# The last chunks of an RWKV-7 recurrence: state decayed ahead of its terms, and four steps in another order

## The reference, cut to what matters

```python
def step(state, inp):
    r_t, w_t, k_t, v_t, a_t, b_t = inp
    sa = jnp.einsum('bhvk,bhk->bhv', state, a_t)
    state = (state * w_t[:, :, None, :] + sa[..., None] * b_t[:, :, None, :]
             + v_t[..., None] * k_t[:, :, None, :])
    return state, jnp.einsum('bhvk,bhk->bhv', state, r_t)
...
y = rms_norm((b_gate * y).reshape(bsz, seq, CONV_GROUPS, HEAD_DIM), out_gain)   # short convolution
...
y = jnp.concatenate([y_rwkv, y_conv, y_attn], axis=-1)
x = x + y @ w_o[l]
```

## Time and profile before

| | us |
|---|---|
| median of 3 runs | 1580.93 |
| lowest, highest | 1580.54, 1581.57 |
| the profiled execution, its time | 1580.65 |
| the profiled execution, its span | 1578.8 |
| PE busy | 1555.1 (98%) |
| DVE busy | 1264.2 (80%) |
| ACT busy | 1073.8 (68%) |

### The profile page before, as it was taken

One profiled execution on the slowest core, in us unless ns is written; L12 is line 12 of the kernel. 1 busy time (PEld: TensorE's weight loads), 2 busy tenths in 40 slices (PEclk: granted clock), 3 DMA queues, 4 the chain that ended last, 5 costly groups with the idle time before them and its releaser, 6 DMA issues.

```text
span 1578.8 us, 28727 instructions
## 1 busy us (share of the span) xinstructions
PE 1555.1 (98%) x10958; PEld 1359.9 (86%) x10958; DVE 1264.2 (80%) x1440; ACT 1073.8 (68%) x1323; POOL 80.2 (5%) x82
## 2 busy tenths in 40 slices
PE   8999999999999998999999999999999999999997
PEld 8988999999999887888888888888888888888886
DVE  5686754444567866999999999999999999999996
ACT  5545444444446455788888888888888888888885
POOL 0022000000000400000000000000000000000000
PEclk9999999999999999999999999999999999999999
DMA  8700655555344008999999999999999999999994
GB/s 313 234 2 3 220 186 184 186 187 187 122 163 152 3 17 307 359 377 361 391 393 361 389 393 362 394 390 358 393 389 359 393 390 359 392 391 358 390 379 158
DMA packets 189944, 447.76 MB, mean 284 GB/s; under 512 B 8208, under 2 KB 10784, under 8 KB 189728
## 3 DMA queue, kind: packets, MB, share of 16 engines
q1 hardware_dynamic: 186480, 434.46, 75.5%
q0 software_dynamic: 2688, 9.44, 2.7%
q10 hardware_dynamic: 688, 2.62, 0.5%
HBM read 438.63 MB, written 6.29 MB: 282 GB/s over the span
## 4 chain that ended last, share of the span: by engine, by line
PE 96%; DVE 2%; ACT 1%; issue 1%; DMA 0%; POOL 0%; SPq 0%; DVEq 0%; ACTq 0%; POOLq 0%
PE bank L789 28%; PE bank L791 27%; PE bank L790 27%; PE bank L770 9%; PE bank L1465 2%; ACT w_hi L1544 0%; DMA ring<-in_w_in 0%; PE bank L960 0%; PE bank L810 0%; DVE w_lo L2239 0%; PE bank L1428 0%; PE bank L1214 0%; DVE w_lo L1986 0%; PE bank L1105 0%; POOL out L740 0%
## 5 line engine op out<-in xcount | busy, mean ns | idle before, releaser
L1544 ACT ACTIVATE w_hi<-ring 128x1024 fp32r<-128x1024 f32 x812 | 858.6, 1061 | 334.5 <-PE bank L791 324.5
L2239 DVE TENSOR_TENSOR w_lo<-ring,w_hi 128x1024 fp32r<-128x1024 f32 x672 | 814.4, 1224 | 62.6 <-ACT w_hi L1544 12.9
L789 PE MATMUL bank<-w_hi,acts_hi 128*128 128x512 f32 (+1 forms) x1376 | 539.7, 392 | 3.5 <-DVE w_lo L2239 3.4
L791 PE MATMUL bank<-w_hi,acts_lo 128*128 128x512 f32 (+1 forms) x1376 | 533.6, 388 | 0.0
L790 PE MATMUL bank<-w_lo,acts_hi 128*128 128x512 f32 (+1 forms) x1376 | 532.8, 387 | 0.0
L789 PEld LDWEIGHTS bank<-w_hi,acts_hi 128*128 128x128 f32 x1376 | 258.9, 188 | 55.4 <-DVE w_lo L2239 4.5
L791 PEld LDWEIGHTS bank<-w_hi,acts_lo 128*128 128x128 f32 x1376 | 258.7, 188 | 53.8
L790 PEld LDWEIGHTS bank<-w_lo,acts_hi 128*128 128x128 f32 x1376 | 259.1, 188 | 50.8
L789 PE MATMUL bank<-acts_hi,w_hi 128*128 128x256 f32 x884 | 252.4, 286 | 2.7 <-DVE acts_lo L2146 1.7
L790 PE MATMUL bank<-acts_lo,w_hi 128*128 128x256 f32 x884 | 250.1, 283 | 0.0
L791 PE MATMUL bank<-acts_hi,w_lo 128*128 128x256 f32 x884 | 250.1, 283 | 0.0
(11 more groups left out here) (247 smaller groups left out, 1112.6 us busy)
## 6 DMA issues: line engine op xcount, KB each, us to landing
ring<-in_moe_wg SPq DMA_DIRECT2D x112, 1024.0 KB, 7.1
ring<-in_moe_wu SPq DMA_DIRECT2D x112, 1024.0 KB, 7.5
ring<-in_moe_wd SPq DMA_DIRECT2D x112, 1024.0 KB, 7.1
ring<-in_w_in SPq DMA_DIRECT2D x24, 1024.0 KB, 7.8
ring<-in_dense_wg SPq DMA_DIRECT2D x14, 1024.0 KB, 5.2
ring<-in_dense_wu SPq DMA_DIRECT2D x14, 1024.0 KB, 5.1
ring<-in_dense_wd SPq DMA_DIRECT2D x14, 1024.0 KB, 4.9
ring<-in_w_o SPq DMA_DIRECT2D x8, 1024.0 KB, 7.7
```

Source lines behind the costliest of these rows:

```text
L789: pe.matmul(out_, a_hi, b_hi, start=first, stop=False, **kw)
L791: return pe.matmul(out_, a_lo, b_hi, start=False, stop=final, **kw)
L1544: return act.activation(o, i, ACT.Copy, **kw)
L2239: TT(w_lo[:, q, :], raw, w_hi[:, q, :].bitcast(F32), ALU.subtract).then_inc(lo_ready, 1)
```

## The change

The state is multiplied by its decay into `state_tmp` ahead of time (`decay_state`, before the add of u), and when the terms are there, three STTs, one for each pair of heads, make terms x decay + that product. `times_v(l, 5)` goes behind the b-u terms of border 2. The conv root goes from behind output_squares(4) to right behind the last exponentials, and its reciprocal from behind keep_output(5) to behind add_u(1). `spread_conv` writes bank 4 instead of bank 3 and no longer waits for `o_ready`; `scale_conv` reads there. `add_u(3)` goes ahead of `keep_output(l, 5)`. Nothing else is changed; the state's values are the same but for rounding.

```diff
@@ TensorE, recurrence @@
                 state_terms(2, tok_k, tok_v, True, False)
-                times_v(l, 5)
                 pe.wait_ge(u_ready, 3 * l + 2)
                 state_terms(2, tok_b, u_tok, False, True).then_inc(st_done, 1)
+                times_v(l, 5)
@@ TensorE, spread_conv @@
                 pe.wait_ge(conv_ready, l + 1)
-                pe.wait_ge(o_ready, HEADS * l + HEADS)
...
-                            last = mm(bank[3][e * HD:(e + 1) * HD, t * T + b * P:t * T + (b + 1) * P],
+                            last = mm(bank[4][e * HD:(e + 1) * HD, t * T + b * P:t * T + (b + 1) * P],
@@ ScalarE, recurrence @@
                 exponentials(l, 5)
+                act.wait_ge(conv_kept, l + 1)
+                act.activation(conv_rms, conv_rms, ACT.Sqrt).then_inc(conv_root, 1)
...
                 output_squares(l, 4)
-                act.wait_ge(conv_kept, l + 1)
-                act.activation(conv_rms, conv_rms, ACT.Sqrt).then_inc(conv_root, 1)
                 keep_cross(2)
@@ VectorE, recurrence @@
                     if c:
-                        then(TT(state_tmp, terms, state, ALU.add))
-                        TT(state, state_tmp, end, ALU.mult).then_inc(st_ready, 1)
+                        for i in range(NRT):
+                            last = STT(state[:, i, :], terms[:, i, :], w65[:, i, c, C:C + 1], state_tmp[:, i, :],
+                                       ALU.mult, ALU.add)
+                        last.then_inc(st_ready, 1)
...
+                def decay_state(c):
+                    dve.wait_ge(st_ready, 3 * l + c)
+                    then(TT(state_tmp, state, w65[:, :, c, C:C + 1].to_broadcast([P, NRT, HD]), ALU.mult))
...
-                               bank[3][:, i * T:(i + 1) * T], ALU.mult, ALU.mult)
+                               bank[4][:, i * T:(i + 1) * T], ALU.mult, ALU.mult)
 
                 state_update(0)
+                decay_state(1)
                 add_u(1)
+                dve.wait_ge(conv_root, l + 1)
+                dve.reciprocal(conv_rms, conv_rms).then_inc(conv_ready, 1)
                 state_update(1)
-                dve.wait_ge(st_ready, 3 * l + 2)
+                decay_state(2)
                 add_u(2)
                 state_update(2)
+                dve.wait_ge(st_ready, 3 * l + 3)
+                add_u(3)
                 keep_output(l, 5)
-                dve.wait_ge(conv_root, l + 1)
-                dve.reciprocal(conv_rms, conv_rms).then_inc(conv_ready, 1)
-                add_u(3)
                 scale_conv(0).then_inc(conv_out, 1)
```

## The result

| | us |
|---|---|
| before, median of 22 runs | 1580.96 (1579.49 to 1583.29) |
| changed, median of 22 runs | 1583.45 (1582.23 to 1585.85) |
| ratio | 1.0016, 95% interval 1.0009 to 1.0022 (1.4 to 3.5 us) |
| the profiled execution, its time and span | 1584.49, 1582.6 |

The account below looks back on a forecast made before the run. TensorE was taken to bound the kernel, carrying the chain for 96% of the span. The first output tile 0.39 us later in each of two layers gave +0.78, so 1581.7 against the 1580.93 median; range 1579.2 to 1583.3.

Parts of the forecast that it names:

- X: Start of from_state(3) on TensorE, 148.06 before; forecast at 147.21, 0.85 us earlier.
- the STTs: VectorE's state update: three 128x64 operations from PSUM at 0.68 us together, replacing an add and a multiply of 0.76.
- decay, root and bank: Decay ahead of add_u, earlier conv root on ScalarE, spread in bank 4: costed at nothing, keep_cross(1) held 0.05 at most.
- Here the gain is lost: add_u(3) ahead of keep_output(5) on VectorE: o_ready 0.43 us later, although from_state(3) starts 0.85 earlier.
- the term of 0.39 per layer: First output tile on TensorE starts 0.39 us later, 152.77 instead of 152.38, through ScalarE's queue behind o_ready.
- rival B: TensorE's clock halves behind the new pause: 1.4 us per layer, 1584.5 for both, 1583.1 for one; chance 0.08.
- The new pause, 2.0 us behind 64x64 products, lies between: TensorE's pause ahead of the first output tile, between a 1.3 us pause without clock fall and 3.26 us with one.
- Rival A: ScalarE doesn't hold the first output tile, which follows from_state(3): 0.85 us earlier per layer, 1579.2 us; chance 0.11.
- Rival C: The three STTs take 1.44 us together, so from_state(3) starts at 148.70: 3.8 us in all, 1584.7; chance 0.04.
- The rule on small operations: Fixed latency exposed between VectorE instructions: three STTs would take 0.84 us without overlap, each layer ending 0.29 later.
- the row of L2217: Trace row of same-size VectorE operations, 0.28 us for one, 0.48 for two, from which 0.68 for three was taken.

Follow-up runs that it names:

- experiments 1 to 3: 1: changed kernel, keep_output(5) ahead of add_u(3) again, 1578.77; 2: kernel before with add_u(3) first and bank-4 spread, 1584.97; 3: changed kernel, bonus operations ahead of output_squares(5), 1579.39.
- experiments 9 and 10: 9: the changed kernel again, 1583.71; 10: the changed kernel with four unused identity products in TensorE's pause ahead of the first output tile, 1582.75.
- 6: The kernel before with the decay ahead and the three STTs, nothing else changed: 1580.27 beside 1581.39, ratio 0.9996.
- 7: The changed kernel with keep_output(5) ahead of add_u(3), three bonus operations ahead of output_squares(5), spread_conv ahead of the last outputs with v: 1579.59, ratio 0.9987.
- 11: The kernel before with add_u(3) ahead of keep_output(5), the spread in bank 4, and four identity products filling TensorE's pause: 1585.07, ratio 1.0025.

## Why the prediction was wrong

**Right: the mechanism.** X was forecast at 147.21 and came at 147.18; the STTs at 0.68 and came at 0.67; decay, root and bank cost nothing that shows (keep_cross(1) starts 0.02 later). "Here the gain is lost" was the step that decided, and experiments 1 to 3 show it: the swap alone costs 1.35 per layer, without it the tile is 0.77 earlier than before (0.85 was X's gain), and a shorter queue saves it even with the swap. The chain of waits of before did not name ScalarE at all; the prediction found it by working out how little it had in hand, 0.04 us.

**Undersized: the term of 0.39 per layer.** It measured 0.52. The reciprocal of keep_output was put 0.08 before the end of add_u(3), by the pair at 147.65 and 147.93; it starts 0.59 behind the start of an add that takes 0.56, so 0.03 after its end. That is 0.11, of which an add_u(3) 0.03 earlier than forecast gives some back: `o_ready` came 0.52 later than before and not 0.43. The other 0.04 of the 0.13 arose between the squares and the tile. In both layers: 1.04 instead of 0.78.

**Failed: the clock behind the new pause, put at nothing in the sum and given a chance of 0.08 as rival B.** "The new pause, 2.0 us behind 64x64 products, lies between" was the step. The pause was 2.2 and was followed by a fall in 6 of 10; 2 of the 3 profiled executions of the changed kernel had one, in one layer each. Its price was put at 1.4 per layer and is 1.1 to 1.2. The forecast should have been 1.04 plus some fraction of 2.4, and the range should have reached past falls in both layers. The evidence that kept the chance low was the earlier trace rows, clock 1.00 behind the 1.3 us pause at 610 to 612. That row was one draw: in 7 of the 14 executions profiled in this study the same pause was followed by a fall (5.46 us or more instead of 3.84). One execution can show that a fall happens, never that there is none in the others. The Trainium skill's rule (TensorE: Matmul & The Clock Gate, Part 1), that idleness halves the clock, points the way of these falls; the runs agree in 6 of the 10 pauses.

**The sum.** Late tiles 1.04, and 0.96 for the open pause by the medians of experiments 9 and 10, are 2.0 of the 2.5 measured, inside 1.4 to 3.5. The remaining 0.5 is less than the medians of the kernel before differ by between sets of runs (1580.72 to 1581.68). By the means it is gone: 1.04 and 1.5 make 2.5, as far apart as the means of the 22 runs of each kernel are (1583.65 and 1581.14). How the clock's part divides between the pause and falls elsewhere is open beyond the profiled executions. Rival A fell: the tile did not follow X. Rival C fell at 0.67. The rule on small operations (the Trainium skill, VectorE: DVE Perf Modes, TRN2 errata), taken without any overlap, would have given 0.84 for the three; the row of L2217 was right to 0.01.

## What to carry to other kernels

When an operation moves ahead of another on one engine, follow the one that was pushed back: its event, everything queued behind whoever waits for it, and how little that queue has in hand, even where the chain of waits doesn't name it. A gain that leaves TensorE waiting in one piece instead of several can cost clock as well, as the 2.2 us here did where 0.83 did not, so price the pause it makes, not only the sum of idle time. And look at several executions before taking a clock of 1.00 behind a pause as a fact about the pause.

## What was not expected of the hardware

The clock's falls come and go between executions of the same program. Behind the 1.29 us pause of the routing they came in 7 of 14 profiled executions, behind 2.2 us pauses in 6 of 10, and never behind those of 1.04 or less ahead of the output tile. The fall at 183 us was missing in four of the 14 (6, 7, 10 and 11). The later start of the four with a fall in layer 0 is a hint, and no more, that the pause alone doesn't decide. Each fall costs 1.1 to 2.9 us here, and among the runs of one kernel the longer ones have the lower mean clock, so falls make much of the 3.6 to 3.8 us over which 22 runs spread. Four unused products of the identity in the gap went with a clock of 1.00 behind all six filled pauses, at no cost to the tile.
